# VectorE takes every second scaled row of an expert tile's later slots

## The reference

```python
def block(xb):                                    # 128 tokens
    ...                                           # product keys: 8 heads x 16 experts of 16384
    w = jax.nn.softmax(top_s, axis=-1)
    hid = jnp.einsum('td,thkd->thk', xb, u[eidx])
    act = jax.nn.gelu(hid, approximate=False) * w
    return jnp.einsum('thk,thkd->td', act, v[eidx])
```

## Time and profile before

| | |
|---|---|
| median of 3 runs (lowest, highest) | 4641.23 us (4624.23, 4641.85) |
| the profiled execution, its span | 4631.82 us, 4628.8 us |
| TensorE busy | 3646.6 us, 79% of the span |
| VectorE busy | 2619.4 us, 57% |
| ScalarE busy | 2381.7 us, 51% |
| GpSimd busy | 1405.1 us, 30% |
| mean granted clock of TensorE | 0.846 |
| bytes moved by gathers | 1143.02 MB of 1390.11 MB |

### The profile page before, as it was taken

One profiled execution on the slowest core, in us unless ns is written; L12 is line 12 of the kernel. 1 busy time (PEld: TensorE's weight loads), 2 busy tenths in 40 slices (PEclk: granted clock), 3 DMA queues, 4 the chain that ended last, 5 costly groups with the idle time before them and its releaser, 6 DMA issues.

```text
span 4628.8 us, 54190 instructions
## 1 busy us (share of the span) xinstructions
PE 3646.6 (79%) x19165; PEld 2770.8 (60%) x19165; DVE 2619.4 (57%) x5586; ACT 2381.7 (51%) x4295; POOL 1405.1 (30%) x1160
## 2 busy tenths in 40 slices
PE   7999799994788998776777778798878666666666
PEld 5666576663676666754555566566666555555555
DVE  3565345125667775634674555498542666756744
ACT  3222211013877454754555576656473566666665
POOL 0000000002233232424444323333331445555554
PEclk9999899997999999887888889999888666666666
DMA  2000222346889999989999988999998999999998
GB/s 78 28 28 28 94 83 87 105 122 249 313 331 381 354 369 345 416 342 364 366 342 381 354 336 294 353 411 386 364 413 287 391 389 418 416 420 419 418 406 334
DMA packets 293641, 1390.11 MB, mean 300 GB/s; under 512 B 35112, under 2 KB 100328, under 8 KB 153094
## 3 DMA queue, kind: packets, MB, share of 16 engines
q0 software_dynamic: 158720, 1143.02, 62.1%
q1 hardware_dynamic: 134669, 243.89, 15.2%
HBM read 1353.22 MB, written 33.95 MB: 300 GB/s over the span
## 4 chain that ended last, share of the span: by engine, by line
PE 39%; DMA 24%; ACT 11%; DVE 10%; issue 3%; POOL 1%; SPq 1%; ACTq 0%; DVEq 0%; POOLq 0%
DMA p_ring<-in_peer_uv,p_idx 17%; PE psum L1947 10%; PE psum L1309 7%; DVE p_ring L2015 4%; PE psum L1388 4%; ACT p_ring L1981 4%; PE psum L1313 3%; DMA t_w<-in_w_query 3%; PE psum L929 3%; PE psum L1354 2%; ACT L1976 1%; DVE group L1541 1%; DMA group<-in_x_all 1%; ACT p_act_w L1978 1%; PE psum L944 1%
## 5 line engine op out<-in xcount | busy, mean ns | idle before, releaser
L1927 POOL DMA_INDIRECT p_ring<-in_peer_uv,p_idx x1088 | 1332.9, 1225 | 2574.9 <-PE psum L1947 1901.9
L1947 PE MATMUL psum<-ident,p_ring 128*128 128x128 f32 x8704 | 1485.7, 329 | 773.5 <-ACT p_ring L1981 773.2
L1947 PEld LDWEIGHTS psum<-ident,p_ring 128*128 128x128 f32 x8704 | 1237.3, 171 | 1054.7 <-ACT p_ring L1981 969.2
L2015 DVE CUSTOM_DVE_ANT_0 p_ring<-p_ring,p_xn 128x1024 f32<-128x1024 f32 x1088 | 1324.5, 1220 | 860.3 <-DMA p_ring<-in_peer_uv,p_idx 859.4
L1981 ACT ACTIVATE p_ring<-p_ring,p_act_w 128x1024 f32<-128x1024 f32 x1088 | 1249.7, 1149 | 35.5
L1976 ACT ACTIVATE p_gl<-p_hid 128x1 f32<-128x1 f32 x1088 | 217.0, 199 | 998.8 <-DVE p_hid L2015 997.2
L1309 PE MATMUL psum<-group,t_w 128*128 128x384 f32 (+1 forms) x1344 | 443.0, 473 | 0.2 <-DMA t_w<-in_w_conv 0.2
L1978 ACT ACTIVATE p_act_w<-p_gl,p_w 128x1 f32<-128x1 f32 x1088 | 320.5, 295 | 35.3
L1388 PE MATMUL psum<-group,t_w 128*128 128x384 f32 (+1 forms) x768 | 280.3, 509 | 61.4 <-DMA t_w<-in_w_query 60.2
L1309 PEld LDWEIGHTS psum<-group,t_w 128*128 128x128 f32 x1344 | 246.9, 192 | 125.9 <-issue 5.3
L1388 PEld LDWEIGHTS psum<-group,t_w 128*128 128x128 f32 x768 | 150.3, 208 | 137.7 <-DMA t_w<-in_w_query 63.6
(11 more groups left out here) (315 smaller groups left out, 4025.0 us busy)
## 6 DMA issues: line engine op xcount, KB each, us to landing
t_w<-in_w_merge SPq DMA_DIRECT2D x72, 768.0 KB, 8.3
t_w<-in_w_query SPq DMA_DIRECT2D x48, 576.0 KB, 7.7
p_ring<-in_peer_uv,p_idx POOLq DMA_INDIRECT x1088, 9.6
group<-in_cache_kT SPq DMA_DIRECT2D x64, 256.0 KB, 7.0
group<-in_cache_v SPq DMA_DIRECT2D x64, 256.0 KB, 3.5
t_w<-in_w_conv SPq DMA_DIRECT2D x24, 512.0 KB, 7.7
t_w<-in_w_outs SPq DMA_DIRECT2D x24, 512.0 KB, 7.8
t_w<-in_w_fox SPq DMA_DIRECT2D x24, 512.0 KB, 21.4
```

The lines of the kernel that those rows point to most:

```text
L1927: pool.indirect_dma_start(ring[:, at % RING, :], None, io["peer_uv"], bass.IndirectOffsetOnAxis(ap=idx[:, u, c:c + 1], axis=0)).then_inc(r ...
L1947: last = pe.matmul(acc[u][:, k * P:(k + 1) * P], ring[:, at % RING, D + k * P:D + (k + 1) * P], ident[:, :], start=(c == 0 and k % 4 == 0) ...
L2015: dve.tensor_tensor_reduce(out=ring[:, g, 0:D], in0=ring[:, g, 0:D], in1=xn[:, u, :], scale=1.0, scalar=0.0, op0=ALU.mult, op1=ALU.add, ac ...
```

## The change

In slots with c of 28 or more and c even (`by_dve`), VectorE multiplies the row's second half with its weight and adds it to `v_sum`, a 128x1024 sum in SBUF (the place of `hbuf`). It does so behind the dot product of the next slot. ScalarE's scaling and TensorE's eight transposes of that slot are gone. The tile's first such operation has no sum to add to and waits for the store of the tile before. GpSimd waits for `part_ok` where such a slot had the place in the ring. At the tile's end TensorE adds `v_sum` with two more matrix products; in the last tile `fold` adds its two halves of the partitions. Since `hbuf` holds the sum now, h is loaded into half of `cand`, behind the choice that uses it. `lf_tok` moves into `top` to make room, so the first choice waits for its stores.

```diff
+def by_dve(c):
+    return c >= 28 and c % 2 == 0
+def summed(at, dve):
+    return sum(by_dve(x % EXPERTS) == dve for x in range(at))
...
-        yT = s[:, 0:KD, :]
+        yT, h_in, v_sum = s[:, 0:KD, :], s[:, KD:2 * KD, :].rearrange("p c n -> p (c n)"), hbuf
+        fold = m.sb("p_fold", [P, NS])
...
# choose_dve
             if t:
                 dve.wait_ge(s_loaded, 16 * t)
+            else:
+                dve.wait_ge(f_stored, after(16 * fox_stores(1, 0)))
# finish_sp
-            sp.wait_ge(stored, after(16 * t))
-            sp.dma_start(hbuf[0:n, :], io["h_scratch"][t * P:t * P + n, :]).then_inc(h_loaded, 16)
+            if t < 8:
+                sp.wait_ge(idx_ok, after(t + 2))
+            sp.dma_start(h_in[0:n, :], io["h_scratch"][t * P:t * P + n, :]).then_inc(h_loaded, 16)
# finish_pe, behind the products that add h
+            pe.wait_ge(part_ok, after(summed(slots_to(t + 1), True)))
+            for hf in range(2):
+                pe.matmul(acc[u][0:n, hf * 512:(hf + 1) * 512], ident[:, :] if n == P else fold[:, :], v_sum[:, hf * 512:(hf + 1) * 512],
+                          start=False, stop=False, skip_group_check=True)
# GpSimd
-                        pool.wait_ge(row_free, after(at - RING + 1))
+                        dve = by_dve((at - RING) % EXPERTS)
+                        pool.wait_ge(part_ok if dve else row_free, after(summed(at - RING + 1, dve)))
# TensorE
-                    pe.wait_ge(v_ok, after(at + 1))
-                    for k in range(KD):
+                    if not by_dve(c):
+                        pe.wait_ge(v_ok, after(summed(at + 1, False)))
+                        for k in range(KD):
...
# ScalarE, behind gelu and the weight
+                    if not by_dve(c):
+                        act.wait_ge(act_ok, after(at + 1))
...
# VectorE, behind the dot product of slot c
+                    if c and by_dve(c - 1):
+                        b = (at - 1) % RING
+                        dve.wait_ge(act_ok, after(at))
+                        dve.wait_ge(part_ok, after(summed(at - 1, True)))
+                        if summed(at - 1, True) == summed(slots_to(t), True):
+                            dve.wait_ge(stored, after(16 * t))
+                            dve.tensor_scalar(v_sum[:, :], ring[:, b, D:2 * D], act_w[:, b:b + 1], None, ALU.mult).then_inc(part_ok, 1)
+                        else:
+                            dve.scalar_tensor_tensor(v_sum[:, :], ring[:, b, D:2 * D], act_w[:, b:b + 1], v_sum[:, :],
+                                                     ALU.mult, ALU.add).then_inc(part_ok, 1)
```

More of the change, by code:

```diff
@@ L694, in stage_experts @@
         heads, causal, fb = m.sb("f_heads", [P, 2, 8]), m.sb("f_causal", [P, P]), m.sb("f_fb", [P, 1])
-        lf_tok = m.sb("f_lf_tok", [P, NT, 8])
+        lf_tok = top[:, :, :].rearrange("p h k -> p (h k)")[:, 0:NT * 8].rearrange("p (t h) -> p t h", h=8)
         fnmax, frsum, frinv = m.sb("f_nmax", [P, 2]), m.sb("f_rsum", [P, 2]), m.sb("f_rinv", [P, 2])
@@ L728, in stage_experts @@
         stored, tails_stored = m.sem("p_stored"), m.sem("c_tails_stored")
-        (consts, halved, row_free, dot_ok, gl_ok, act_ok, v_ok, yT_ok, acc_ps, y_ok, link, idx_ok, wd_ok, we_ok, w_ok, fss, fsd, frs) = (
+        (consts, halved, row_free, part_ok, dot_ok, gl_ok, act_ok, v_ok, yT_ok, acc_ps, y_ok, link, idx_ok, wd_ok, we_ok, w_ok, fss, fsd, frs) = (
             m.sem("p_" + x) for x in (
-                "consts halved row_free dot_ok gl_ok act_ok v_ok yT_ok acc_ps y_ok link idx_ok wd_ok we_ok w_ok fss fsd frs").split())
+                "consts halved row_free part_ok dot_ok gl_ok act_ok v_ok yT_ok acc_ps y_ok link idx_ok wd_ok we_ok w_ok fss fsd frs").split())
         (g_z, v_z, th_ok, mg_ok, o_ps, res_ok, ss_ok, sd_ok, rs_ok, xn_ok, xt_ps, xt_ok, q_ps, q_ok, s_ps, s_part, s_ok, t_link, res_part) = (
@@ L1695, in finish_act @@
             yield base + 4
-            act.wait_ge(row_free, after(slots_to(t + 1)))
+            act.wait_ge(row_free, after(summed(slots_to(t + 1), False)))
             act.activation(yT[:, :, :], acc[u].rearrange("p (k n) -> p k n", k=KD), ACT.Copy).then_inc(yT_ok, 1)
@@ L1944, in _ @@
                     at = slots_to(t) + c
-                    pe.wait_ge(v_ok, after(at + 1))
-                    for k in range(KD):
[L1947 to L1950, removed]
+                    if not by_dve(c):
+                        pe.wait_ge(v_ok, after(summed(at + 1, False)))
+                        for k in range(KD):
+                            last = pe.matmul(acc[u][:, k * P:(k + 1) * P], ring[:, at % RING, D + k * P:D + (k + 1) * P], ident[:, :],
+                                             start=(c == 0 and k % 4 == 0), stop=(c == slots - 1 and k % 4 == 3), is_transpose=True,
+                                             skip_group_check=True)
+                        last.then_inc(row_free, 1)
                     for x in ends + trunk:
@@ L1978, in _ @@
                     act.activation(act_w[:, g:g + 1], gl[:, g:g + 1], ACT.Copy, scale=w[:, u, c:c + 1]).then_inc(act_ok, 1)
-                    act.wait_ge(act_ok, after(at + 1))
-                    act.wait_ge(row_loaded[g], 16 * (at // RING + 1))
-                    act.activation(ring[:, g, D:2 * D], ring[:, g, D:2 * D], ACT.Copy, scale=act_w[:, g:g + 1]).then_inc(v_ok, 1)
+                    if not by_dve(c):
+                        act.wait_ge(act_ok, after(at + 1))
+                        act.wait_ge(row_loaded[g], 16 * (at // RING + 1))
+                        act.activation(ring[:, g, D:2 * D], ring[:, g, D:2 * D], ACT.Copy, scale=act_w[:, g:g + 1]).then_inc(v_ok, 1)
                     for x in work:
@@ L1995, in _ @@
             dve.wait_ge(zeroed, after(1))
+            dve.tensor_tensor(fold[:, :], ident[:, 0:NS], ident[:, NS:P], ALU.add)
             dve.wait_ge(s_stored[0], after(16 * 8))
```

2 lines of the change are left out of this document (1 added, 1 removed).

## The result

The changed kernel takes 4639.62 us in the median of 20 runs, the kernel before 4625.28 in 20 runs beside them: ratio 1.0034, 95% interval 1.002 to 1.0048. So it is 9 to 22 us slower, which lies within the 0.5% that I had called no change. The profiled executions have spans of 4628.8 and 4647.0 us, +18.2; the sum of the prediction was +22. The small difference is made of large ones of both signs, and several terms of the prediction's sum were wrong.

What follows compares the result with a forecast made beforehand. No engine bounds the whole; TensorE holds 39% of the chain of waits, and transfers limit the second part. Terms 49 - 28 - 7 - 8 + 4 + 10 + 2 = +22 on 4631.8 give 4654; predicted 4660 us, range 4595 to 4722.

Steps and rivals of the forecast that it cites:

- signs of being wrong: New operation not near 1.28 us, full stretches not growing, long VectorE waits for a weight, first part's clock outside 0.85 to 0.92.
- Tile 4, +24: Slots 28 to 67: VectorE is full, 20 sums of 1.20 us cost 24.0 us, and 5.1 us idle stay as gaps.
- Tile 5, +17: From slot 70: VectorE, busy 119.30 of 136 us, gets 24 sums more; +12 at least, +18 with gaps.
- Tiles 6 and 7, +8: VectorE's sums overfill stretches at 3925 to 4078 and 4283 to 4384 us: +3 in tile 6, +5 in tile 7.
- Attention passes, -28: Tiles 0 and 3: scores of 14 even-slot units start sooner without transposes in front, 2 us each; 0 to -62.
- TensorE nearly full, -7 and -8: Fewer transposes shorten tile 1's slots 28 to 71 by 7 us and tile 5's slots 28 to 67 by 8.
- Cached keys +4: Tiles 1 to 3: sums lengthen GpSimd's 7 waits for VectorE's scan, mostly covered by other transfers; 0 to 13 us.
- the clock +10: At 2656 to 2938 us, fewer transposes lower TensorE's clock from 0.89 to 0.75, so 16 units' scores take longer.
- The wait for the weight, 0: VectorE's new wait for ScalarE's weight costs nothing, since the weight is ready 0.7 us behind the preceding slot's dot product.
- The rest, +2: Two more matrix products per tile join the tile's sum, nearly all beside gathers; +2 us.
- Rival C: TensorE's clock falls in the whole first part, deciding under about 0.85; at 0.80 it costs 80 us, 4724; chance 0.13.
- Rival D: GpSimd issues gathers late, standing until VectorE's sum ends; 0.8 us for a third of 275 issues, +73, 4727; chance 0.08.

Runs made afterwards that it cites:

- e7: As e2, but VectorE's operation works on one column instead of 1024, with the same waits; ratio 1.0002 to the kernel before.
- e2: The changed kernel with VectorE's sums only in tiles 4 and 5, every second slot from 28; ratio 1.0117 to the kernel before.
- e5: Sums only in tiles 0, 1 and 3; ScalarE still does a scaling in the summed slots of tiles 0 and 3; ratio 0.9937 to the kernel before.
- e6: Sums only in tiles 0, 1 and 3; TensorE makes eight identity transposes in tiles 0 and 3's summed slots; ratio 0.9892 to the kernel before.
- e9: As e5, and TensorE also waits for that scaling but makes no transposes there; ratio 0.9983 to the kernel before.
- e3: The changed kernel with VectorE's sums only in tile 2, every second slot from 52; ratio 1.0051 to the kernel before.
- e4: As e3, but TensorE makes eight identity transposes in each summed slot, keeping its load; ratio 1.0008 to the kernel before.

## Why the prediction was wrong

The sum came out near (+22, measured +18 by the spans and +14 by the medians), but by errors that cancel: the eight stretches that it speaks of made +3, and 15 us came from elsewhere. That the total is near is luck. The steps that failed are the price of the attention passes, the place where the clock falls, and the gaps of tile 4; two of the signs of being wrong that I had named came as well, a clock of the first part below 0.85 and long waits for a slot's weight. The sum also stood at the edge of 0.5%. On such an edge the chance of no change (0.34) should have been above that of slower (0.42). The 4660 is 20 us above the measured 4639.62, and 16 of them are a second error: it was put on a median of three runs, and that of 20 is 16 us lower.

- **Tile 4, +24: measured +19.** The failed step is that the 5.1 us of VectorE's idle stay as gaps. They were filled to 1.3: VectorE's busy time grew by 23.1, the stretch by 19.3. The floor that I had given as an end (18.9) was the answer. In e7 VectorE is busy 128.62 us in the same 130.7, so the gaps were room that the gathers left, not a price of dependent instructions that stays.
- **Tile 5, +17: measured +20. Tiles 6 and 7, +8: measured +4.** The mechanism stood, and e2 and e7 show it for tile 5.
- **Attention passes, -28: measured -49.** This step failed in its mechanism. The scores were to come sooner where a unit's own slot has no transposes, at even slots only. In tile 0 the group at slots 33 to 45, all at odd slots, gained 2.3 us as well, and the group at even slots, 56 to 68, 3.1 (38.5 to 35.4), half a us a unit and not 2. No engine seemed full over the whole pass; ScalarE was, in the units' slots (e5 against e6), and TensorE in the projections', for whose slots I had no term. In tile 3 the wait of TensorE for a scaled row, which the sum had, was the larger part of the price (e9 against e5).
- **TensorE nearly full, -7 and -8: measured -8 in tile 1.** Of tile 5's query stretch nothing can be said: its slots 28 to 68 took 170.2 us before and 171.2 after, but 158 to 177 in the runs where no slot of it was changed.
- **Cached keys +4 and the clock +10: measured +17 at the cached keys.** The failed step is where the clock falls. I had put it at the attention pass of tile 3, whose clock went from 0.89 to 0.87; it fell in tile 2, from 0.85 to 0.66, and with it went the score products of the cached keys, as e3's rows show (837 ns a score product in the changed kernel, 621 before). The Trainium skill, "TensorE: Matmul & The Clock Gate", section "Part 1: The HAM clock gate", has the low clock as the default, which activity lifts; e4, where useless transposes hold 0.82, agrees. Why tile 3 kept its clock with as many transposes gone, the changed kernel shows in part: its projections (second row, slots 64 to 73) run at 0.98, its score units (first row, 52 to 64) at 0.77.

```profile
2657.20:2698.60 41.40, 28.86 (x136) 21.09 (x136) 32.30 (x73) 24.54 (x44) 13.47 (x13) 0.77 0.99 403
2698.60:2728.60 30.00, 23.46 (x168) 21.05 (x168) 24.97 (x52) 16.97 (x36) 13.07 (x9) 0.98 0.77 268
```

- **The wait for the weight, 0: measured 59 us of waiting, price not found.** In the full stretches of tiles 4 and 5 it doesn't occur (0.3 us at most in one wait). In the query stretch VectorE's wait for gathers went from 122.0 to 54.0 us, so the new wait stands in the place of old ones. e7 has the same wait (46.7 us) without the sums' time, and its query stretch took 169.0 us. That the stretch didn't get the 8 us that I expected there may be the wait's price; within its spread it can't be told.
- **The rest, +2**: no run measures it by itself.
- **Rival C** had the right form and the wrong price. The clock of the first part fell to 0.83, below the 0.85 from which I let it decide, and the first part got 1.4 us shorter: only one stretch, tile 2's, is shown to have paid for it. (The 275 slots in its price and in D's are 267, 50 in each of tiles 0 to 4 and 17 in tile 5; that changes neither much.) **Rival D** came in its mechanism and not in its price: GpSimd's busy time in the first part rose from 862.88 to 916.37 us, 53 of the 73 that I had counted, yet where the slots gained, the DMA share rose (to 0.98 in tiles 0 and 1), so no price of late issues shows there. In the last part little of it was left to come: I had taken an issue of 0.94 us as the usual one, but from 3870 us on the median is 1.72 us before (first row) and after (second).

```profile
L1927 POOL DMA_INDIRECT p_ring<-in_peer_uv,p_idx x286: 932/1720/1981, 3870.4 to 4596.9; - x143
```

```profile
L1946 POOL DMA_INDIRECT p_ring<-in_peer_uv,p_idx x286: 932/1722/2744, 3870.0 to 4598.0; - x143
```

## What to carry to other kernels

Cut a window where the kind of work changes: a pass in which no engine is full may be made of pieces in each of which another one is. Two things at their limit in one row, as ScalarE and the DMA engines here, are told apart by giving the load back to one of them. When work moves between engines, choose its places one stretch at a time by what is full there; the same kind of edit cost 0.3% when made everywhere and gained 1.9% where ScalarE or TensorE held the slots and VectorE had room. And where the granted clock falls when work is taken away, give useless work back in that stretch, as e4 does: if the stretch gets faster, the work that was taken away had kept the clock up.

## What the hardware showed that I had not expected

TensorE with 27% fewer instructions can be busy longer: 234.93 us for 878 in e3 against 218.88 for 1210 before, at a clock of 0.61 against 0.85. Eight transposes that compute nothing, in every second slot, shorten that stretch from 315.5 us (298.4 in the changed kernel) to 291.1.
